# One fused pass for a decoder's last norm, 512-column PLE tiles, and split keys for a weight load

## The reference

```python
for i in range(DEPTH):                       # DEPTH = 2
    h = h + mixer_i(rmsnorm(h, norm_mix[i]))
    y, tail = conv_ffn(rmsnorm(h, norm_ffn[i]), ...)
    h = h + y
    gate = jax.nn.sigmoid(rmsnorm(h, norm_ple[i]) @ ple_w_gate[i])   # 1024 x 1024
    h = h + gate * (p[i] @ ple_w_proj[i])                            # 256 x 1024
out = rmsnorm(h, norm_final)
```

## Time and profile before

| | before |
|---|---|
| median of the timed runs | 2936.56 us (2 runs, 2935.91 and 2937.2) |
| the profiled execution | 2672.52 us, its span 2671.0 us |
| spans of the 8 cores in it | 2657.3 to 2671.0 us |
| mean granted PE clock | 0.875 to 0.877 of full on every core |
| busy: PE, DVE, ACT, POOL | 2074.0, 1220.4, 912.5, 321.4 us |
| DMA | 141.24 MB, mean 53 GB/s |

### The profile page before, as it was taken

How to read it: one execution, slowest core, us unless ns; L and a number is a source line. 1 busy time by engine, 2 the same in 40 slices (tenths; PEclk the granted TensorE clock), 3 DMA queues, 4 the chain that set the end, 5 groups by cost and what they waited for, 6 DMA issues and landing times.

```text
span 2671.0 us, 39315 instructions; the slowest of 8 cores (2657.3 to 2671.0 us)
## 1 busy us (share of the span) xinstructions
PE 2074.0 (78%) x12496; PEld 1136.9 (43%) x12496; DVE 1220.4 (46%) x2801; ACT 912.5 (34%) x1939; POOL 321.4 (12%) x676
## 2 busy tenths in 40 slices
PE   0577699997578899984277669999856887999974
PEld 0356244445245344443156524444433453444452
DVE  0245544355543544455145554433555434443466
ACT  0466222225333222233166632222433423222243
POOL 0664000000000000000265400000000000000000
PEclk9888799998678899997589779999877778999986
DMA  9240444451401434364300053443432000343202
GB/s 163 47 63 1 71 64 63 64 80 33 78 1 29 75 61 71 59 103 88 94 1 1 1 82 48 64 64 56 54 69 46 1 11 1 63 65 61 43 7 68
DMA packets 118875, 141.24 MB, mean 53 GB/s; under 512 B 21266, under 2 KB 91154, under 8 KB 118676
## 3 DMA queue, kind: packets, MB, share of 16 engines
q0 software_dynamic: 82048, 115.42, 27.9%
q1 hardware_dynamic: 36628, 23.32, 3.3%
HBM read 244.11 MB, written 10.03 MB: 95 GB/s over the span
## 4 chain that ended last, share of the span: by engine, by line
PE 66%; DVE 12%; DMA 6%; issue 5%; ACT 5%; POOL 5%; DVEq 0%; ACTq 0%; POOLq 0%; SPq 0%
PE PS L392 66%; DVE SB L380 5%; DMA SB<-xT 4%; POOL SB L372 3%; ACT SB L354 3%; DVE SB L357 2%; DVE SB L549 2%; DMA yT<-SB 2%; ACT L354 2%; POOL SB L357 1%; ACT SB L384 1%; DMA SB<-wsT 1%; DVE SB L727 0%; DVE SB L850 0%; DVE SB L386 0%
## 5 line engine op out<-in xcount | busy, mean ns | idle before, releaser
L392 PE MATMUL PS<-SB 128*128 128x256 bf16 (+3 forms) x12496 | 2074.0, 323 | 581.9 <-DVE SB L380 168.4
L392 PEld LDWEIGHTS PS<-SB 128*128 128x128 bf16 x12496 | 1136.9, 102 | 1518.9 <-issue 787.2
L357 DVE TENSOR_TENSOR SB<-SB,PS 128x512 f32<-128x512 f32 (+5 forms) x936 | 494.8, 548 | 622.2 <-ACT SB L354 357.5
L384 ACT ACTIVATE SB<-PS 128x512 bf16<-128x512 f32 (+6 forms) x424 | 160.4, 407 | 903.4 <-PE PS L392 500.7
L354 ACT ACTIVATE SB<-PS,SB 128x512 f32<-128x512 f32 (+4 forms) x511 | 261.3, 531 | 257.4 <-PE PS L392 167.7
L380 DVE SCALAR_TENSOR_TENSOR SB<-SB 128x256 f32<-128x256 f32 (+4 forms) x656 | 274.8, 467 | 48.1 <-DMA yT<-SB 26.8
L354 ACT ACT_TABLE_LOAD x150 | 192.4, 1283 | 250.5 <-PE PS L392 199.1
L354 ACT ACTIVATE SB<-SB 128x256 bf16<-128x256 f32 (+6 forms) x531 | 200.0, 434 | 126.2 <-PE PS L392 112.4
L354 ACT ACTIVATE SB<-PS 128x256 f32<-128x256 f32 (+5 forms) x322 | 117.5, 391 | 208.1 <-PE PS L392 108.1
L357 DVE TENSOR_TENSOR SB<-SB 128x256 f32<-128x256 f32 (+7 forms) x220 | 110.8, 509 | 144.5 <-ACT SB L354 101.6
L397 POOL DMA_DIRECT2D SB<-ffn_w_up x48 | 42.5, 886 | 1044.0 <-PE PS L392 923.0
(11 more groups left out here) (21 smaller groups left out, 63.9 us busy)
## 6 DMA issues: line engine op xcount, KB each, us to landing
SB<-ffn_w_up POOLq DMA_DIRECT2D x48, 1024.0 KB, 8.9
SB<-ffn_w_down POOLq DMA_DIRECT2D x24, 1024.0 KB, 8.8
SB<-lru_w_in POOLq DMA_DIRECT2D x2, 4096.0 KB, 31.0
SB<-xT SPq DMA_DIRECT2D x8, 1024.0 KB, 6.1
SB<-gm_w_in POOLq DMA_DIRECT2D x2, 4096.0 KB, 31.1
SB<-ple_w_gate POOLq DMA_DIRECT2D x4, 2048.0 KB, 14.2
yT<-SB SPq DMA_DIRECT2D x8, 1024.0 KB, 4.5
SB<-lru_w_out POOLq DMA_DIRECT2D x2, 2048.0 KB, 37.6
```

What stands on the lines that cost most here:

```text
L357: emit(eng, lambda e: e.tensor_tensor(out=out.ap, in0=a.ap, in1=b.ap, op=op), R=[a, b], W=[out])
L384: emit("act", lambda e: e.activation(out=out.ap, in_=in_.ap, func=AF.Copy), R=[in_], W=[out])
L392: emit("pe", lambda e: e.matmul(ps.ap, lhsT=lhsT.ap, rhs=rhs.ap, start=start, stop=stop), R=[lhsT, rhs] + list(R), W=[ps])
```

## The change

1. The PLE uses the tiles of 512 columns (`ptiles = ffn_tiles`) and scratch of twice the size: two tiles in place of four in the first group, three in place of five in the second (512, 512, 64).
2. The final rmsnorm is no stage of its own. In layer 1 a tile's final norm and output DMA (`p_final`) are written after the body of the next tile, the last one after the last body; they use 512 columns too, and scratch of their own (`sqs2` with two buffers, `sd2`). `issue_next_block` of that layer is written after them.
3. `w_lin` is loaded in two halves by columns under two keys (R1a, R1ag), the half needed first ahead of `w_la` and `w_lx`, the other one behind them; `w_lout` has a key R1bo.

```diff
-        def load_mixer0():
-            load_mat(R1a, w_lin, "R1a")
+        def load_lru_weights():
+            dma("pool", R1a.v(None, (1024, 2048)), w_lin[:, 1024:2048].rearrange("(k p) n -> p k n", p=128), key=KEY["R1a"])
             load_mat(R1b_wa, w_la, "R1b")
             load_mat(R1b_wx, w_lx, "R1b")
-            load_mat(R1b_wout, w_lout, "R1b")
+            dma("pool", R1a.v(None, (0, 1024)), w_lin[:, 0:1024].rearrange("(k p) n -> p k n", p=128), key=KEY["R1ag"])
+            load_mat(R1b_wout, w_lout, "R1bo")
...
-                sqs = [T(mem, [256], BF16) for _ in range(3)]
-                sd = T(mem, [256], F32)
-                xns = [T(mem, [KC, 256], BF16) for _ in range(2)]
-                thb = [T(mem, [256], F32) for _ in range(2)]
-                tb = [T(mem, [256], F32) for _ in range(2)]
+                sqs = [T(mem, [512], BF16) for _ in range(3)]
+                sd = T(mem, [512], F32)
+                sqs2 = [T(mem, [512], BF16) for _ in range(2)]
+                sd2 = T(mem, [512], F32)
+                xns = [T(mem, [KC, 512], BF16) for _ in range(2)]
+                thb = [T(mem, [512], F32) for _ in range(2)]
+                tb = [T(mem, [512], F32) for _ in range(2)]
...
+                ptiles = ffn_tiles
...
+                def p_final(ti):
+                    c0, n, kind = ptiles[ti]
+                    rmsnorm(c0, n, "nfin", [hv(c, c0, n) for c in range(KC)], (sqs2, sd2))
                     gcol = G["p0"] + c0 if kind == "p" else SEQ
                     hvr = Hreg.v(None, (c0, c0 + n))
                     dma("sp", yv[:, :, gcol:gcol + n], hvr, key=KEY["H"])
                     final_bufs.append(KEY["H"])
+
+                p_pro(0)
+                for ti in range(len(ptiles)):
+                    p_body(ti, range(0, 2))
+                    if ti + 1 < len(ptiles):
+                        p_pro(ti + 1)
+                    p_body(ti, range(2, KC))
+                    if l == 1 and ti > 0:
+                        p_final(ti - 1)
+                if l == 1:
+                    p_final(len(ptiles) - 1)
+                issue_next_block()
```

More of the change, by code:

```diff
@@ L467, in dcol @@
             return DER.v(r, (c, c + 1))
-        KEY = {n: Buf("key_" + n) for n in ("R1a", "R1b", "slot0", "slot1", "P", "H")}
+        KEY = {n: Buf("key_" + n) for n in ("R1a", "R1ag", "R1b", "R1bo", "slot0", "slot1", "P", "H")}
         def load_w(dst_T, kidx, src_rows_ap, key):
@@ L484, in build_program, with load_mixer0 @@
         XNall = T(mem, [KC, 1088], BF16, off=R1b_off)
-        def load_mixer0():
-            load_mat(R1a, w_lin, "R1a")
+        def load_lru_weights():
+            dma("pool", R1a.v(None, (1024, 2048)), w_lin[:, 1024:2048].rearrange("(k p) n -> p k n", p=128), key=KEY["R1a"])
             load_mat(R1b_wa, w_la, "R1b")
             load_mat(R1b_wx, w_lx, "R1b")
-            load_mat(R1b_wout, w_lout, "R1b")
+            dma("pool", R1a.v(None, (0, 1024)), w_lin[:, 0:1024].rearrange("(k p) n -> p k n", p=128), key=KEY["R1ag"])
+            load_mat(R1b_wout, w_lout, "R1bo")
+        def load_mixer0():
+            load_lru_weights()
         def load_mixer1_in():
@@ L1028, in build_program @@
                 arena_reset()
-                sqs = [T(mem, [256], BF16) for _ in range(3)]
-                sd = T(mem, [256], F32)
-                xns = [T(mem, [KC, 256], BF16) for _ in range(2)]
-                thb = [T(mem, [256], F32) for _ in range(2)]
-                tb = [T(mem, [256], F32) for _ in range(2)]
+                sqs = [T(mem, [512], BF16) for _ in range(3)]
[5 more added lines that the diff above has]
+                tb = [T(mem, [512], F32) for _ in range(2)]
                 bj = (gi * 2 + l) * (NSL + 1) + NSL
                 slot = slots[bj % 2]
+                ptiles = ffn_tiles
+                yv = yT.rearrange("(c p) n -> p c n", p=128)
                 def p_pro(ti):
-                    c0, n, kind = mix_tiles[ti]
+                    c0, n, kind = ptiles[ti]
                     xn = xns[ti % 2]
@@ L1075, in build_program @@
                     final_bufs.append(KEY["H"])
+                p_pro(0)
[9 more added lines that the diff above has]
+                issue_next_block()
+                dump(l * 3 + 2, DBG_GROUP, gi, ng)
+            else:
                 continue
```

## The result

The changed kernel's median is 2623.32 us (11 runs). Timed beside each other, its time is 0.9812 of the time before, 95% interval 0.9798 to 0.9826: 50 us less of 2672, or 1.9%. That it is faster is clear of the noise; whether by 2% the interval leaves open. Executions of either kernel can be disturbed and some per cent longer, the comparisons leave those out, and the two runs that stood for the kernel before ahead of the prediction (2935.91 and 2937.2) were such, while its undisturbed ones take 2669.6 to 2674.8 us.

What follows compares the result with a forecast made beforehand. The rmsnorm's chain through ACT and DVE was taken to bound the PLE, PE stalling once per tile. 9.9 + 11.7 + 4 + 1 + 15.5 + 0.7 - 5 = 38 us, taken as 35 off the timed median: 2902 us, range 2876 to 2928.

Steps and rivals of the forecast that it cites:

- The anchor: Whole kernel: timed median 264 us longer than the profiled execution, so 38 us became 35 for a slower PE, giving 2902.
- The first group: Layer 0 PLE gains 9.9 us; layer 1 PLE and final norm take 98.1 us instead of 113.65, gaining 15.5.
- the terms 9.9, 4 and 15.5: First-group gains in us: layer 0 PLE 9.9, gMLP start 4, layer 1 PLE with final norm 15.5.
- The second group: Layer 0 PLE gains 11.7 us; layer 1 PLE with final norm takes 117.1 instead of 117.8, gaining 0.7.
- Into the gMLP: At the gMLP's start wsT is issued earlier: 4 us gained in the first group, 1 us in the second.
- The key split: At the LRU's start x holds, not weights, so splitting w_lin's load costs and gains 0, from -2 to +2 us.
- If x came earlier, the half's wait would matter: At the LRU's start: the second half of w_lin waits for the first, which would matter with x earlier; no size given.
- The clock: In eight norms or so, squares keep PE under half busy for 4 to 5 us; 5 us taken off (0 to 10).
- The hidden norm: Final norm hidden behind the next body: 25 us more leave the end, time near 2877; chance 0.08.
- The clock rival: Clock falls in each wide PLE norm and stays at 0.50: slower, up to 3038 us; chance 0.08.
- Little comes of it: Slower output DMAs, squares, first x load or PE leave a gain of 5 to 18 us, near 2925; chance 0.17.
- the seven switches of the prediction: Some seven root table switches leave the path, two per PLE less one; by the page's price some 10 us more gain.

Runs made afterwards that it cites:

- e12: e7 with the key split undone (w_lin in one piece, w_lout under the key R1b): 0.9537 of the time before, 18.5 us more than e7.
- e7: Changed kernel with exact pages, a key per x and output tile, and lng, lnb, wsf at the arena's end: 0.9489 of before, 85.6 us less than the changed kernel.

## Why the prediction was wrong, and where it was right

**The anchor: wrong, and this decides.** The step is "The timed median is 264 us longer than that execution ... so I take 35: 2902 us". The sum was made against 2672.5, the two timed runs said 2936.56, and I moved the sum onto them. The kernel before takes 2669.6 to 2674.8, so the anchor was some 263 us too high, five times the change itself. Two runs that agree with each other and not with the profiled execution show that one of the two is not the kernel's usual time; no row said which. The range should have held both (2672.5 - 38 = 2634 as well), or the text should have given the gain as a share. No run tests the 3 us that the step took off for a slower PE. And a change under 2% can well be told from none here: the interval reaches 0.14% to either side.

**The first group: right.** PE started 9.85 us after the squares (9.9 said), the PLE took 56.5 (55.5), the first final norm from its squares to the output DMA 17.0 (16.8), the DMAs 12.45 and 7.48 (12.4 and 7.9). The 1.0 us too much in the PLE is there by the second tile's squares, at 19.65 (18.5 said): the first 20 matmuls took 9.64 us where the sum has 8.8 (5.39 and 3.4), since from 1163.81 to 1167.64 they start 0.43 us apart at a granted clock of 0.50. From the FFN's end to the x load it is 99.1 us (98.1). Over the cores 28.5 us are gained by there; the terms 9.9, 4 and 15.5 make 29.4.

**The second group: right in kind, small in size.** The PLE of layer 0 gained 11.8 (11.7), and the second body ended 58.5 us after the first squares, as said. From FFN 1's end the whole took 114.6 on the slowest core (117.1 said), since each 2 MB DMA took 6.9 us and not 7.9. Over the cores this last stage gained 2.1 (0.7). For the output DMA I had 6.9 and 8.9 as bounds and took the middle. The lower one was right: 256 KB in 2.6 and 1 MB in 4.44 lie on a line with 6.87. The Trainium skill (DMA: Bandwidth & Descriptors, Anatomy of one DMA) has that line for another queue's DMAs, 2.0 us and the bytes over 436 GB/s. It gives 6.8 us for 2 MB, an estimate, and these rows agree.

**Into the gMLP: right in the first group, low in the second.** 4.5 us less idle time (4 said), and 2.7 for 1.

**The key split: right.** 0, with the reason given: x held the start. e12 shows the sentence "If x came earlier, the half's wait would matter" with the sign turned: the split then gains 18.5 us, because the shared keys' waits are longer than the half's.

**The clock: wrong.** The step took 5 us off. The stage's mean is 0.88 for 0.89 and the whole span's is 0.877 to 0.882 for 0.875 to 0.877. Beyond the 1 us above no loss is seen. The rows of before were read too narrowly: there the clock was at 0.50 not only in the first burst but, behind the stall of 2.37 us, again from 1187.70 to 1190.50, and behind the next one from 1205.00 to 1206.50. These two bursts of 32 matmuls took 5.24 us and 5.32, where 32 at the last burst's rate are 3.5:

```profile
1203.74 5.32 PE L392 MATMUL PS<-SB 128*128 128x256 bf16 x32 [2.21 <-DVE SB L380]
...
1219.86 10.20 PE L392 MATMUL PS<-SB 128*128 128x256 bf16 x92 [2.29 <-DVE SB L380]
```

In the changed kernel the clock is 1.00 behind the stall of 1.46 us and to the end of the stage. So in this stage the wide tiles kept the clock up where the term had them lose it. With that term at 0 the sum is 43 against 48 measured; the other 5 are 2 in the second gMLP, 1.4 at the end and small gains in the LRU and FFN stages, less 0.9 in the first group.

**The rivals.** The hidden norm did not come: the body waits 6.92 us for the DMA, as the order showed. The clock rival did not come, by the clocks just given. "Little comes of it" did not either. The drain of 1.38 us that the Trainium skill (ScalarE: Activation LUTs, What ACT_TABLE_LOAD costs) has behind the table load is not there, as before; in the timeline of the changed kernel the root starts 0.01 us after the load:

```profile
1173.60 1.28 ACT L354 ACT_TABLE_LOAD   x1 [0.66 <-PE PS L392]
1174.89 0.69 ACT L354 ACTIVATE SB<-PS,SB 128x512 f32<-128x512 f32 x1
```

Of table loads there are 136 where there were 150; the 14 that went are the seven switches of the prediction, each with its way back.

## What to carry to other kernels

When the profiled execution and the timed runs differ by more than the change is worth, make the sum against the profile and forecast for both anchors. Before a transfer is hidden behind other work, look for what that work waits on: here the fused body waited for an output DMA because of a tracker of first-to-last byte and one counter for many DMAs. Taking both away, in the whole kernel, was worth 75 us, more than the change itself, while either alone gave 29 or nothing. Even then the fused order cost 6.5 us, because its work stood in the queues of DVE and ACT ahead of the next norm. A change that brings nothing may be waiting for another bound to go: the key split went from 0 to 18.5 us.

## What the runs showed of the hardware

- A 2 MB output DMA took 6.86 to 7.48 us with little beside it and 12.45 beside the next block's load; 1 MB took 4.44 and 256 KB 2.6. Two of 1 MB in a row thus take 8.88 us and one of 2 MB 6.87, so each output DMA that goes saves about 2 us.
- Eight squares of 512 columns took 4.25 us with three scratch buffers. With two they took 5.09 in the first final norm of a group, where PE's clock was still 1.00 at the start, and 5.50 in the second, at a clock of 0.50, where they go in pairs, one every 1.45 us. The third buffer is thus worth some 0.8 to 1.3 us a norm where the squares stand on the path. In the second norm of the first group ACT reads:

```profile
1214.80 1.15 ACT L354 ACTIVATE SB<-SB 128x512 bf16<-128x512 f32 x2 [0.31 <-PE PS L392]
1216.25 1.15 ACT L354 ACTIVATE SB<-SB 128x512 bf16<-128x512 f32 x2 [0.31 <-PE PS L392]
```

- With the false waits on x gone, the first 60 us of e7 have a DMA share of 1.03 at 179 GB/s, and a weight's transfer that is issued at 3.45 us lands 42.20 us later. The x loads flow beside the weights there. That these bytes together are the bound is argued from the share of 1.03, and no run took bytes away.
- In the first group's PLE of layer 1 in the kernel before, the granted clock fell from 1.00 to 0.50 behind a stall of 2.37 us and, a little later, behind one of 2.21, and stayed at 1.00 behind one of 2.29. So the length of the stall alone does not tell which level comes.
